# Query projection of the expert routing as products of rounded parts, and a longer pick on GpSimd

## The reference

```python
def peer(h, w_q, sub_keys, u_tab, v_tab):
    q = (h @ w_q).reshape(B, S, PEER_HEADS, 2, PEER_HALF)             # 8 heads, 2 x 128
    s = jnp.einsum('bshpd,hpnd->bshpn', q, sub_keys)                   # 128 keys for each half
    v1, i1 = lax.top_k(s[..., 0, :], PEER_TOPK)                        # 16 of 128
    v2, i2 = lax.top_k(s[..., 1, :], PEER_TOPK)
    cand = (v1[..., :, None] + v2[..., None, :]).reshape(B, S, PEER_HEADS, 256)
    cv, ci = lax.top_k(cand, PEER_TOPK)
    e1 = jnp.take_along_axis(i1, ci // PEER_TOPK, axis=-1)
    e2 = jnp.take_along_axis(i2, ci % PEER_TOPK, axis=-1)
    g = jax.nn.softmax(cv, axis=-1)
    ...   # then sum over the picked experts of g * gelu(h . u[e]) * v[e]
```

## Time and profile before

| what | us |
|---|---|
| median of three runs | 2474.6 |
| the profiled execution | 2471.42 |
| its span, first to last instruction | 2470.2 |
| TensorE busy | 2341.4 (95% of the span) |
| VectorE busy | 1917.5 (78%) |
| ScalarE busy | 1157.1 (47%) |
| GpSimd busy | 153.6 (6%) |

### The profile page before, as it was taken

The page is one execution under the profiler, slowest core; times in us unless marked ns, Lnnn a source line. Parts: engine busy times, 40 slices in busy tenths (PEclk is TensorE's granted clock), DMA queues, the critical chain, the costliest instruction groups (busy, mean ns, idle before and its releaser), DMA issues. The chain is left out here.

```text
span 2470.2 us, 37755 instructions
## 1 busy us (share of the span) xinstructions
PE 2341.4 (95%) x11671; PEld 1913.4 (77%) x11671; DVE 1917.5 (78%) x4361; ACT 1157.1 (47%) x2034; POOL 153.6 (6%) x172
## 2 busy tenths in 40 slices
PE   7998998899898999999999989898899999999997
PEld 5775466667787888888888856687788888888886
DVE  5677778757997788888888856599877777777776
ACT  5674247242285444444444435415844444444443
POOL 0000000000351000000000000014400000000000
PEclk9999999999999999999999999999999999999999
DMA  6524640653213667666777641222155555555553
GB/s 257 183 104 141 238 159 22 228 199 115 77 35 122 227 251 261 254 254 247 258 254 255 253 167 69 88 84 69 38 194 192 194 190 187 188 192 193 190 187 136
DMA packets 144615, 429.31 MB, mean 174 GB/s; under 512 B 15231, under 2 KB 21375, under 8 KB 144511
## 3 DMA queue, kind: packets, MB, share of 16 engines
q1 hardware_dynamic: 144510, 428.08, 48.8%
HBM read 426.99 MB, written 1.05 MB: 173 GB/s over the span
## 5 line engine op out<-in xcount | busy, mean ns | idle before, releaser
L3396 PE MATMUL bank<-v_parts,weighted_high 128*128 128x512 f32 x1952 | 531.2, 394 | 6.0 <-DVE weighted_low L3536 6.0
L3382 PE MATMUL bank<-h_t_parts,u_t_high 128*128 128x512 f32 x1824 | 450.5, 389 | 0.0
L3396 PEld LDWEIGHTS bank<-v_parts,weighted_high 128*128 128x128 f32 x1952 | 352.8, 190 | 70.8 <-issue 7.5
L3382 PEld LDWEIGHTS bank<-h_t_parts,u_t_high 128*128 128x128 f32 x1824 | 342.3, 188 | 71.1
L3476 ACT ACTIVATE activated<-activated 128x256 f32<-128x256 f32 x228 | 95.6, 419 | 476.5 <-DVE activated L3524 476.5
L3457 ACT ACTIVATE u_t_high<-u_ring 128x1024 fp32r<-128x1024 f32 x228 | 241.3, 1058 | 163.3 <-DMA u_ring<-in_peer_u 161.9
L3396 PE MATMUL bank<-v_parts,weighted_low 128*128 128x512 f32 x976 | 302.8, 391 | 0.0
L3511 DVE TENSOR_TENSOR u_t_low<-u_ring,u_t_high 128x1024 fp32r<-128x1024 f32 x228 | 278.7, 1222 | 30.1 <-ACT u_t_high L3457 26.8
L3518 DVE TENSOR_TENSOR v_parts<-v_ring,v_parts 128x1024 fp32r<-128x1024 f32 x242 | 294.4, 1217 | 3.3 <-ACT v_parts L3464 3.3
L3464 ACT ACTIVATE v_parts<-v_ring 128x1024 fp32r<-128x1024 f32 x242 | 255.1, 1054 | 71.1 <-PE bank L3396 70.9
L3385 PEld LDWEIGHTS bank<-h_t_parts,u_t_low 128*128 128x128 f32 x1824 | 248.8, 190 | 17.8
(11 more groups left out here) (593 smaller groups left out, 3543.7 us busy)
## 6 DMA issues: line engine op xcount, KB each, us to landing
v_ring<-in_peer_v SPq DMA_DIRECT2D x244, 512.0 KB, 3.3
u_ring<-in_peer_u SPq DMA_DIRECT2D x228, 512.0 KB, 4.5
panel<-in_l_w_in SPq DMA_DIRECT2D x15, 2048.0 KB, 8.1
late_tiles<-in_ada_w SPq DMA_DIRECT2D x54, 512.0 KB, 4.3
mod_ring<-in_ada_w SPq DMA_DIRECT2D x42, 512.0 KB, 4.7
panel<-in_peer_w_q SPq DMA_DIRECT2D x8, 2048.0 KB, 7.7
panel<-in_l_w_out SPq DMA_DIRECT2D x4, 2560.0 KB, 8.8
early_u<-in_peer_u SPq DMA_DIRECT2D x20, 512.0 KB, 3.4
```

The lines of the kernel that those rows point to most:

```text
L3382: nc.tensor.matmul(banks[2 + k][:, :], UTH[:, k, j, :], H2[:, j, :, :].rearrange("p a s -> p (a s)"), start=(j == 0), stop=False, skip_gro ...
L3396: last = nc.tensor.matmul(banks[4 + 2 * t + half][:, :], w[:, t * P:(t + 1) * P], v[k][:, half * 512:(half + 1) * 512], start=opens and n ...
```

## The change

The change touches the routing stage alone, in both layers.

- **Projection.** Head 0 stays as it was. For heads 1 to 7 each float32 product becomes three products of rounded parts: high weights by high rows, high weights by low rows, low weights by high rows. The rows' parts existed before.
- **Weights' parts.** The high part of a head's weights (`peer_q_high`, 2048 elements per partition, a ring of three) is made by a ScalarE copy for heads 2 to 7 (`round_head`) and by a GpSimd copy for head 1. The low part is made by a GpSimd subtraction for all seven heads (`low_head`), written over the panel.
- **Scores** of head h - 1 are taken after the ninth product of head h.
- **Pick.** After its multiplication GpSimd adds the 16 columns of each row into 8 and then into 4. VectorE sums the 4 that are left.
- **Keys.** The conversion of the indices moves from VectorE to ScalarE (`copy_keys`); GpSimd waits for it.
- **ScalarE's order.** Heads' roundings and key conversions stand between the copies. After head 7 it converts the keys of head 6, copies two early products, converts the keys of head 7, and copies the other early products.

```diff
@@ tensor
-                    for h in range(H):
-                        p = ps[h // 2]
-                        wait_panel(pe, p)
+                    ...   # head 0 as before
+                    pe.wait_ge(h_low, 1)
+                    for h in range(1, H):
+                        low = head_panel(h, panel_lows)
                         wait_acc_free(pe, g0 + h)
+                        pe.wait_ge(q_low, h)
                         for half in range(2):
+                            acc, cols = acc_bank(g0 + h)[:, half * S:(half + 1) * S], slice(half * P, half * P + P)
                             for k in range(KD):
-                                last = nc.tensor.matmul(acc_bank(g0 + h)[:, half * S:(half + 1) * S],
-                                                        panel_block(slots[p % 3], h, half, k), HT[:, k, :],
-                                                        start=(k == 0), stop=(k == KD - 1))
-                                if h > 0 and half == 0 and k == 1:
+                                wide = QW[:, h % 3, k, cols]
+                                nc.tensor.matmul(acc, wide, HTH[:, k, :], start=(k == 0), stop=False)
+                                nc.tensor.matmul(acc, wide, HTL[:, k, :], start=False, stop=False)
+                                last = nc.tensor.matmul(acc, low[:, k, cols], HTH[:, k, :], start=False, stop=(k == KD - 1))
+                                if half == 0 and k == 2:
                                     score(h - 1)
@@ scalar
+                    def round_head(h):
+                        wait_panel(act, ps[h // 2])
+                        if h >= 3:
+                            act.wait_ge(acc_ready, g0 + h - 2)
+                        nc.scalar.activation(QW[:, h % 3, :, :], head_panel(h), ACT.Copy).then_inc(q_high, 1)
+
+                    def copy_keys(h):
+                        act.wait_ge(keys_done, h + 1)
+                        nc.scalar.activation(IDF[:, h, :, :, :]..., IDX[:, h, :, :, :]..., ACT.Copy).then_inc(keys_copied, 1)
@@ scalar, in the loop over the heads, after the copy of the queries and after that of the scores
+                        if h == 0:
+                            round_head(2)
                         ...
+                        if g >= 2:
+                            copy_keys(g - 2)
+                        if h == 0:
+                            round_head(3)
+                        elif h + 3 < H:
+                            round_head(h + 3)
-                    for n in range(ROUTED - 2):
+                    copy_keys(H - 2)
+                    copy_early(0)
+                    copy_early(1)
+                    copy_keys(H - 1)
+                    for n in range(2, ROUTED - 2):
                         copy_early(n)
@@ gpsimd
+                    def low_head(h):
+                        nc.gpsimd.tensor_tensor(head_panel(h, panel_lows), head_panel(h), QW[:, h % 3, :, :].bitcast(F32),
+                                                ALU.subtract).then_inc(q_low, 1)
+
+                    def pick(h):
+                        pool.wait_ge(keys_copied, h + 1)
                         pool.wait_ge(decode_in, h + 1)
                         ...
+                        for n, into in ((TOPK // 2, picked), (TOPK // 4, decoded)):
+                            f(nc.gpsimd.tensor_tensor(EQ[:, h, :, 0:n], EQ[:, h, :, 0:n], EQ[:, h, :, n:2 * n], ALU.add), into)
@@ vector
-                                          EQ[:, h, :, :].rearrange("p (a k) j -> p a k j", k=TOPK), AX.X, ALU.add), wait=False)
+                                          EQ[:, h, :, 0:TOPK // 4].rearrange("p (a k) j -> p a k j", k=TOPK), AX.X, ALU.add), wait=False)
@@ vector, in the loop over the steps
-                        if keys:
-                            dve.wait_ge(keys_done, h + 1)
-                            f(v.tensor_copy(IDF[:, h, :, :, :]..., IDX[:, h, :, :, :]...), wait=False)
```

More of the change, by code:

```diff
@@ L176, in build @@
              for i, o in enumerate((PANELS, PANELS + SLOT, WORK_END - SLOT))]
+    panel_lows = [nc.alloc_sbuf_tensor_at(f"panel_low{i}", [P, KD * 512], F32R, offset=o)
+                  for i, o in enumerate((PANELS, PANELS + SLOT, WORK_END - SLOT))]
     MOD_RING = WORK_END - SLOT - 16384
@@ L2865, in peer @@
         UE = zone("early_u", [P, 3, D])
+        QW = zone("peer_q_high", [P, 3, KD, S], F32R)
         UT_AT = RINGS + 36864
@@ L2880, in peer, with head_panel @@
             early_loaded = [sem(f"peer{l}_early_u_loaded{i}") for i in range(3)]
+            q_high, q_low, h_low, keys_copied, picked = (
+                sem(f"peer{l}_{x}") for x in ("q_high", "q_low", "h_low", "keys_copied", "picked"))
+            def head_panel(h, tiles=slots):
+                return tiles[ps[h // 2] % 3][:, 0:KD * 512].rearrange("p (k n) -> p k n", k=KD)[:, :, h % 2 * S:(h % 2 + 1) * S]
             turned_act, turned_dve, turned_there, turn_ahead, turn_behind = turned_rows(rows_in, jobs_in)
@@ L2908, in score @@
                         last.then_inc(scored, 1)
-                    for h in range(H):
-                        p = ps[h // 2]
-                        wait_panel(pe, p)
+                    wait_panel(pe, ps[0])
+                    wait_acc_free(pe, g0)
+                    for half in range(2):
+                        for k in range(KD):
+                            if half == 0:
+                                turn_ahead(pe, k)
+                            last = nc.tensor.matmul(acc_bank(g0)[:, half * S:(half + 1) * S],
+                                                    panel_block(slots[ps[0] % 3], 0, half, k), HT[:, k, :],
+                                                    start=(k == 0), stop=(k == KD - 1))
+                            if half == 0:
+                                turn_behind(pe, k)
@@ L3094, in _ @@
                             done["cand"] = issued_so_far()
-                        if keys:
-                            dve.wait_ge(dve_order, done["keys"])
-                            dve.wait_ge(keys_done, h + 1)
-                            f(v.tensor_copy(IDF[:, h, :, :, :].rearrange("p i t k -> p (i t k)"),
-                                            IDX[:, h, :, :, :].rearrange("p i t k -> p (i t k)")), wait=False)
-                            done["keys"] = issued_so_far()
                         if h >= 4:
```

25 lines of the change are left out of this document (18 added, 7 removed).

## The result

| | before | after |
|---|---|---|
| median of 20 runs, us | 2475.97 | 2503.45 |
| the profiled execution | 2471.42 | 2503.54 |
| its span | 2470.2 | 2502.3 |

The ratio of the runs' means is 1.0091, with a 95% interval of 1.0067 to 1.0114: slower by 0.9%, within the 2% that count as the same. By the medians the ratio is 1.0111, because four of the twenty runs of the kernel before took 2502 to 2510 us, which raises its mean and not its median. The forecast was 2502 us.

A forecast was written before the change was run, and what follows sets the result against it. VectorE was taken to end the routing stage, TensorE 3.7 us behind. +16.4 less 1.8 clock credit gives 14.6 a layer, 29.2 for two: 2500.6 against the profiled execution, 2503.8 against the median, so 2502; range 2476 to 2520.

The forecast's parts named there:

- TensorE's 8.4 us a layer: Projection of seven heads: three products save TensorE 8.4 us, buying nothing by itself; the rival that they are gained: 2455, chance 0.02.
- VectorE without subtractions: VectorE's loop, relieved of conversions and wide sums: last key search at about 646 instead of 652.7, before waits on GpSimd.
- 4.9 us for meetings with the adds: Steps 3 to 7: VectorE's addition waits 0.55 us for a multiplication, its decode 0.4 for GpSimd's first add, five times.
- Four stands of 1.8, 4.5, 3.8, 3.8 us: VectorE's waits for whole GpSimd subtractions of heads 3, 5, 6 and 7, at additions or decode, then pair operations.
- Rival C: VectorE hardly waits for GpSimd: stalls under 3.4 us a layer instead of 18, total 2465 to 2468; chance 0.13.
- D: GpSimd's subtractions dearer, 6.5 us each: 8 to 9 us more a layer, 2517 to 2520; chance 0.12.
- Rival B: VectorE's pair operations (L3035 and kin) don't wait for GpSimd: 6 to 7 us off a layer, 2488 to 2491; chance 0.15.
- The tail: From the last key search at 664: conversion 0.3, copy 0.4, start 0.1, six tiles 20.7, last copy 0.5, ending at 686.0.
- two, two and six: TensorE's ten early tiles split so, with gaps of some 7 to 15 us before the third; the fifth awaits head 7's keys.
- Sum of the stage: The routing stage's end moves from 669.64 to 686.0, +16.4 us a layer.
- The clock's credit of 1.8 us a layer: One-hot stage after routing: TensorE working until the stage's end may start it at 2.4 GHz, 1.8 us back.

The follow-up runs named there:

- e2_no_subtraction: The changed kernel without GpSimd's seven subtractions, the third product reading the high weights instead of the low ones: 2475.8 us.
- e4_old_projection: The changed kernel with the float32 projection of before, keeping the new pick, key conversion and ScalarE order: 2475.06 us.
- e5_projection_only: The changed kernel's projection with the pick and VectorE key conversion of the kernel before: 2496.17 us.
- e3_eight_pieces: The changed kernel with each GpSimd subtraction issued as eight of 256 elements: 2512.33 us.
- e9_one_head_in_parts: The kernel before with keys converted by ScalarE, its last instructions reordered, and head 1 alone in three products from parts made by GpSimd: 2463.85 us.
- e10b_two_sources: The kernel before plus seven unused GpSimd subtractions of 2048 elements, each reading two different tensors: 2498.65 us.

## Why the prediction held

- **TensorE's 8.4 us a layer buy nothing: right.** The products stand 0.117 to 0.119 us apart, and in the first layer e2_no_subtraction and e4_old_projection have their last key search at the same 88.6.
- **VectorE without subtractions: right in kind, 2.3 us too late.** The prediction's 646 plus its 4.9 us for meetings with the adds is 91 from the stage's start; measured 88.6. The adds cost less than I took: the addition lasts 0.69 to 0.86 us instead of 0.45 and the decode 0.45 to 0.47 instead of 0.15, so 0.6 a step, not 0.95. The sum over 4 columns, an estimate of 0.35, took 0.39 to 0.42 us.
- **Four stands of 1.8, 4.5, 3.8, 3.8 us: right.** Measured 1.5, 4.1, 3.8, 3.8, at the places named. Rival C falls with them, and D with subtractions of 4.49 to 4.64 us; I had 4.7. GpSimd was busy for 70.0 us in the stage, as forecast. The Trainium skill ("GPSIMD Engine Reference", Performance versus the Vector engine) has 4497 ns; the trace agrees.
- **Rival B falls.** L3100 (L3035 before), of which no row had shown a meeting, lasts 3.97 us. The Trainium skill ("SBUF — State Buffer", Who interferes with whom) names VectorE instructions with two SBUF inputs, and under conditions casts, as the ones that contend, for the whole of the other's instruction; this trace and the CAST rows of e5_projection_only (3.34 and 4.32 us) agree, and the addition of 8.31 us in e3_eight_pieces, which stood through a dozen of them, goes beyond it.
- **The tail: right.** From the last key search to ScalarE's last copy I had 22.0 us, measured 685.38 - 663.22 = 22.2. My early tiles were to break into two, two and six, with a wait ahead of the fifth. In the second layer they did; in the first they broke into two and eight, at 638.8 and 654.1, because the slow clock that I had put inside the wait filled it. The fifth still began within 1 us of the last key conversion, at about 664.0, and the tail is the same in both layers (22.5 and 22.4).
- **Sum of the stage: 2 us too much.** +16.4 predicted on the path to the end, measured 685.38 - 561.50 against 669.64 - 560.02, +14.3. The excess is mostly the adds' 1.9 and the stands' 0.7, less the 0.8 that I had rounded off.
- **The clock's credit of 1.8 us a layer: the term that failed.** I had argued that a TensorE at work until the stage's end would find the one-hot stage at 2.4 GHz. Windows of the kernel after (start:end, length, busy, PEclk, DMA), which answer to the earlier trace rows:
```profile
663.60:684.50 20.90, 20.90 (x98) 18.39 (x98) 17.38 (x43) 4.18 (x9) 11.53 (x9) 1.00 0.32 101
684.50:691.00 6.50, 2.47 (x17) 1.66 (x15) 4.11 (x12) 3.70 (x10) 3.38 (x5) 0.99 0.36 112
691.00:697.00 6.00, 5.32 (x21) 4.96 (x22) 4.58 (x11) 2.40 (x7) 1.31 (x2) 0.50 0.14 55
```
TensorE was busy without a gap until 684.5, then for 2.47 of 6.5 us among the transposes and one-hots; after that came 6 us at 0.50, the lower level. Before, too, the low stretch came in the one-hots, so work without a gap ahead of them did not spare it; which idle stretch brings it on was not tested. Summed over windows of 2 us, the low stretch is 6.8 us long in the first layer, before and after; in the second it is 10.2 us before and 6.8 after, and yet the stage behind it is not shorter. From the transposes to the end of the expert stage the change takes 1.1 and 0.2 us more, where I had 1.8 less; both lie within the scatter between kernels, so that a credit of 1.8 us could not have been read from these lengths alone; the windows above are what speaks against it.

The two errors have opposite signs, 2.1 a layer too much in the stage (less in layer 2, where it grew by 15.3) and 1.8 of credit that did not come. That the sum hit 2503 so closely is part luck: by the profiled executions the difference is 32.1 us, by the medians 27.5, and the forecast had 29.2. The lower end of the stated range, 2476, had no case behind it: B, the lowest that it was to hold, was worked out as 2488.

**What stays open.** Why, in e3_eight_pieces, one addition of 128 x 128 stood through a dozen pieces while pair operations of 128 x 32 slipped in among others. The two meetings differ in shape, in operation, and in what GpSimd did just before (three heads' pieces in one row, against one head's behind a pick); no run here separates these. Open as well are the 4.9 us of e9_one_head_in_parts and the 3 us between e10b_two_sources and the real subtractions.

## What to carry to other kernels

An idle engine is not free if its instructions keep out those of the engine that sets the pace, as GpSimd's did VectorE's here: price each of its instructions by those of the other that it will meet, in full length, and try it with work that nobody uses before building on it. When an in-order engine is given a new wait, list what is queued behind it; here key conversions ahead of the early copies cost some 4 us a layer. And undo a bundle part by part: one part of this one, the conversions on ScalarE in a better order, was worth 3 to 5 us a layer, hidden under others that cost more.

## What the runs showed of the hardware

- A VectorE instruction that GpSimd holds shows as busy: an addition of 0.45 us for two became 8.47 us with the pieces of e3_eight_pieces. The 2.82 us of idle time beside its name are the wait for scores ahead of it, and no part of this.
- Cutting a GpSimd subtraction in eight costs more than it looks: 4.5 us become 5.6 issued in a row (6.5 where VectorE's instructions got in between), and 6.4 to 7.3 with a wait after each piece.
- A GpSimd subtraction whose two inputs are the same tensor takes 3.60 us for 2048 elements, with two tensors 4.53.
- VectorE's searches ran beside GpSimd's subtractions at full speed: 0.28 us each, as without them.
- It works the other way round too: VectorE's one-hot of 1024 elements at 618.96 us in e3_eight_pieces began 0.08 us ahead of a GpSimd piece, kept its 1.21 us, and the piece took 1.71 us instead of 0.72.
